# Query and key up-projections of the latent attention: columns regrouped while the weights are split, and one rotation in place of four

## What is computed

```python
(cq, ckv, kr, aq, ak, av, qi, ki, wi, rq, rk, rv, rg) = jnp.split(h @ w_in[l], split_at, axis=-1)
q = (rmsnorm(cq, g_q[l]) @ w_uq[l]).reshape(B, S, MLA_HEADS, MLA_NOPE + MLA_ROPE)    # 768 -> 8 heads x (64 + 32)
q_nope = q[..., :MLA_NOPE]
q_rope = apply_rope(q[..., MLA_NOPE:], cos_r, sin_r)
kv = (rmsnorm(ckv, g_kv[l]) @ w_ukv[l]).reshape(B, S, MLA_HEADS, MLA_NOPE + MLA_V)   # 256 -> 8 heads x (64 + 64)
k_nope, v_mla = kv[..., :MLA_NOPE], kv[..., MLA_NOPE:]
k_rope = apply_rope(kr[:, :, None, :], cos_r, sin_r)[:, :, 0]
o_a = mla_attention(q_nope, q_rope, k_nope, k_rope, v_mla)
```

## Time and profile before

| | us |
|---|---|
| median of 3 runs | 1392.13 |
| lowest and highest run | 1390.67 to 1392.34 |
| span of the profiled execution | 1389.4 |
| TensorE busy (share of the span) | 1339.9 (96%) |
| VectorE busy | 855.6 (62%) |
| ScalarE busy | 627.4 (45%) |
| GpSimd busy | 138.0 (10%) |

### The profile page before, as it was taken

How to read it: one execution, slowest core, us unless ns; L and a number is a source line. 1 busy time by engine, 2 the same in 40 slices (tenths; PEclk the granted TensorE clock), 3 DMA queues, 4 the chain that set the end, 5 groups by cost and what they waited for, 6 DMA issues and landing times.

```text
span 1389.4 us, 24758 instructions
## 1 busy us (share of the span) xinstructions
PE 1339.9 (96%) x10446; PEld 1280.1 (92%) x10446; DVE 855.6 (62%) x926; ACT 627.4 (45%) x809; POOL 138.0 (10%) x100
## 2 busy tenths in 40 slices
PE   8999999999989999999999999999999999999998
PEld 6999998789879999999888899999998878999998
DVE  5665557656557555556788765555567975655554
ACT  5443336476524443335534444444464334544442
POOL 2000003100000100002341111000025220200000
PEclk9999999999899999999999899999999989999999
DMA  8565556452225455555434134555644322455550
GB/s 261 171 210 183 183 148 176 128 152 92 90 80 171 145 183 182 181 182 171 146 89 139 61 122 155 184 184 182 178 140 139 111 93 74 169 184 181 181 181 30
DMA packets 179200, 208.83 MB, mean 150 GB/s; under 512 B 24136, under 2 KB 161984, under 8 KB 179008
## 3 DMA queue, kind: packets, MB, share of 16 engines
q1 hardware_dynamic: 178832, 207.73, 47.4%
q10 hardware_dynamic: 304, 0.20, 0.1%
HBM read 206.87 MB, written 1.05 MB: 150 GB/s over the span
## 4 chain that ended last, share of the span: by engine, by line
PE 85%; DVE 7%; ACT 3%; issue 2%; POOL 2%; DMA 1%; POOLq 0%; DVEq 0%; SPq 0%; ACTq 0%
PE bank L1661 74%; PE bank L1964 2%; PE bank L1943 2%; DVE n_lo L1326 2%; POOL scr L831 2%; PE bank L1886 1%; ACT w_hi L901 1%; DVE w_lo L1210 1%; PE bank L1950 1%; DMA raw<-in_ffn_gate_dram 1%; PE bank L1998 1%; PE bank L1937 1%; DVE hT L1347 1%; PE bank L2018 0%; PE bank L1976 0%
## 5 line engine op out<-in xcount | busy, mean ns | idle before, releaser
L1210 DVE TENSOR_TENSOR w_lo<-raw,w_hi 128x2048 fp32r<-128x2048 f32 (+1 forms) x198 | 450.9, 2279 | 297.6 <-ACT w_hi L901 296.8
L1661 PE MATMUL bank<-n_hi,w_hi 128*128 128x256 f32 x1808 | 525.0, 290 | 17.1 <-DVE n_lo L1326 8.2
L1661 PE MATMUL bank<-n_lo,w_hi 128*128 128x256 f32 x1808 | 517.9, 286 | 0.0
L1661 PE MATMUL bank<-n_hi,w_lo 128*128 128x256 f32 x1808 | 517.8, 286 | 0.0
L901 ACT ACTIVATE w_hi<-raw 128x2048 fp32r<-128x2048 f32 (+1 forms) x198 | 370.1, 1873 | 259.3 <-PE bank L1661 258.1
L1661 PEld LDWEIGHTS bank<-n_hi,w_hi 128*128 128x128 f32 x1808 | 351.9, 195 | 26.2 <-DVE n_lo L1326 11.6
L1661 PEld LDWEIGHTS bank<-n_lo,w_hi 128*128 128x128 f32 x1808 | 352.0, 195 | 0.8 <-issue 0.5
L1661 PEld LDWEIGHTS bank<-n_hi,w_lo 128*128 128x128 f32 x1808 | 352.0, 195 | 0.0
L1661 PE MATMUL bank<-hid_hi,w_hi 128*128 128x256 f32 (+1 forms) x1184 | 339.9, 287 | 2.8 <-DVE hid_lo L1618 2.1
L1661 PE MATMUL bank<-hid_lo,w_hi 128*128 128x256 f32 (+1 forms) x1184 | 336.1, 284 | 0.0
L1661 PE MATMUL bank<-hid_hi,w_lo 128*128 128x256 f32 (+1 forms) x1184 | 336.0, 284 | 0.0
(11 more groups left out here) (247 smaller groups left out, 1111.6 us busy)
## 6 DMA issues: line engine op xcount, KB each, us to landing
raw<-in_w_ff_dram SPq DMA_DIRECT2D x64, 1024.0 KB, 5.2
raw<-in_w_in_dram SPq DMA_DIRECT2D x31, 1024.0 KB, 5.4
raw<-in_ffn_gate_dram SPq DMA_DIRECT2D x22, 1024.0 KB, 5.4
raw<-in_ffn_up_dram SPq DMA_DIRECT2D x22, 1024.0 KB, 5.3
raw<-in_ffn_down_dram SPq DMA_DIRECT2D x22, 1024.0 KB, 4.9
raw<-in_w_out_dram SPq DMA_DIRECT2D x12, 1024.0 KB, 5.1
raw<-in_w_uq_dram SPq DMA_DIRECT2D x8, 576.0 KB, 4.1
raw<-in_w_in_dram SPq DMA_DIRECT2D x12, 256.0 KB, 4.0
```

Source lines behind the costliest of these rows:

```text
L1210: V.tensor_tensor(w_lo[:, s % SPLIT, 0:n], raw[:, s % RING, 0:n], w_hi[:, s % SPLIT, 0:n].bitcast(f32), ALU.subtract).then_inc(lo_ready, 1)
L1661: mm = MM(out, stat(k, a), mov(k, b), start=(first and k == 0 and n == 0), stop=(last and k == K - 1 and n == 2), skip_group_check=True)
```

## The change

The query columns are regrouped by the copies that split them, into `w_hi` and `w_lo`: first the 64 unrotated columns of all eight heads (4 blocks of 128), then the 32 rotated ones of all heads (2 blocks). The slabs are cut along the inner dimension instead of by heads: three slabs of two row blocks x 768 columns, and six output blocks, that gather over the three slabs in banks 1 to 3. Banks 1 and 2 hold the unrotated rows, which VectorE scales and writes to `qm` (new step `uqn`, four instructions on 64 rows); bank 3 holds the rotated rows of all heads, which take one rotation (`uqr`) of 128 rows, whose last sum is written as four sums of 32 rows. The `ukv` columns are regrouped in the same manner, keys first: two heads' keys share a block of 128 rows, and the values lie side by side. `proj rg` moves from before `uq` to behind the dsa scores, `uq` 0 to 2 come one after the other, and `idle[0]` is turned off at the first `uq`. Each split of a `uq` or `ukv` slab is two instructions instead of one, on ACT and on VectorE.

```diff
@@ -145,11 +145,10 @@
...
               ("topk", l, 0, 0, 8), ("idx", l, 5), ("idx", l, 6), ("proj", l, "rv"), ("rope", l, "rq"), ("idx", l, 7),
-              ("proj", l, "rg"), ("rtok", -l), ("rope", l, "kr"), ("topk", l, 1, 0, 4), ("uq", l, 0),
-              ("ret", l, 0), ("ret", l, 1), ("ret", l, 2), ("topk", l, 1, 4, 8), ("uq", l, 1), ("rope", l, "uq0"),
-              ("uq", l, 2), ("retv", l), ("rope", l, "uq1")]
-        S += attention(l, [("dsa", 0), ("dsa", 1)], [("retn", l), ("uq", l, 3)], {}, 1)
-        S += [("rety", l), ("rope", l, "uq2"), ("rope", l, "uq3")]
+              ("uq", l, 0), ("rtok", -l), ("rope", l, "kr"), ("uq", l, 1), ("topk", l, 1, 0, 4), ("uq", l, 2), ("uqn", l),
+              ("ret", l, 0), ("ret", l, 1), ("ret", l, 2), ("topk", l, 1, 4, 8), ("rope", l, "uqr"), ("retv", l)]
+        S += attention(l, [("dsa", 0), ("dsa", 1)], [("proj", l, "rg"), ("retn", l)], {}, 1)
+        S += [("rety", l)]
...
@@ -480,14 +479,16 @@
...
             elif kind == "uq":
-                _, l, n = st
+                idle[0] = False
                 slab(st)
-                job(st, of_slab=True)
-                bring(st, [(l, f"uq{n}")], (n + 1) % 2)
+                if st[2] == 2:
+                    for b in range(3):
+                        job(("uqb", st[1], b), b + 1, of_slab=(b == 2))
+                    bring(("uqb", st[1], 2), [(st[1], "uqr")], 1)
...
                 slab(st)
-                for n in range(6):
-                    job(st + (n,), of_slab=(n == 5))
+                for n in range(4):
+                    job(st + (n,), of_slab=(n == 3))
...
@@ -643,9 +644,8 @@
...
                     "kr": (src, 1, MLA_Q, "perm96", c96, krR)}
-            if name.startswith("uq"):
-                n = int(name[2])
-                return src[0:MLA_Q], 2, MLA_Q, con("perm96")[0:MLA_Q, 0:MLA_Q], [x[0:MLA_Q] for x in tab[l]["q"]], qm[0:MLA_Q, 2 * n:2 * n + 2]
+            if name == "uqr":
+                return src, 2, P, con("perm32"), tab[l]["q"], None
...
@@ -726,7 +726,18 @@
...
                 return KD * sum(n for _, n in pieces(key[1], key[2]))
-            return 6 * 192 if key[0] == "uq" else SLAB
+            return 2 * 768 if key[0] == "uq" else SLAB
+
+        def parts(s, to, of):
+
+            key = slabs[s][0]
+            if key not in ("uq", "ukv"):
+                return [(to, of)]
+            a, b = (64, 32) if key == "uq" else (64, 64)
+            to = to.rearrange("p (k c) -> p k c", k=2)
+            of = of.rearrange("p (k h c) -> p k h c", k=2, h=8)
+            return [(to[:, :, 0:8 * a].rearrange("p k (h c) -> p k h c", h=8), of[:, :, :, 0:a]),
+                    (to[:, :, 8 * a:8 * a + 8 * b].rearrange("p k (h c) -> p k h c", h=8), of[:, :, :, a:a + b])]
...
@@ -859,7 +870,7 @@
...
                     pool.wait_ge(r_ready, RN[st] + 1)
-                    scaled(st[1], "q", (con("cos_m"), con("sin_m")), rstd[:, 1, :])
+                    scaled(st[1], "q", (con("cos_i"), con("sin_i")), rstd[:, 1, :])
...
@@ -898,7 +909,9 @@
...
                 n = width(s)
-                nc.scalar.activation(w_hi[:, s % SPLIT, 0:n], raw[:, s % RING, 0:n], ACT.Copy).then_inc(hi_ready, 1)
+                for to, of in parts(s, w_hi[:, s % SPLIT, 0:n], raw[:, s % RING, 0:n]):
+                    last = nc.scalar.activation(to, of, ACT.Copy)
+                last.then_inc(hi_ready, 1)
...
@@ -1081,19 +1094,20 @@
...
                 elif kind == "uq":
-                    _, l, n = st
                     ahead(SL[st])
-                    for r in BEFORE[st]:
+                elif kind == "uqn":
+                    key = ("uqb", st[1], 2)
+                    for r in BEFORE[key]:
                         act.wait_ge(rope_done, RO[r] + 1)
-                    pb = await_bank(act, st)
-                    buf = XSC[(l, f"uq{n}")][1]
-                    nc.scalar.activation(xs[0:MLA_Q, buf, :], pb[0:MLA_Q, :], ACT.Copy, scale=MLA_Q ** -0.5).then_inc(freed(st), 1)
+                    pb = await_bank(act, key)
+                    buf = XSC[(st[1], "uqr")][1]
+                    nc.scalar.activation(xs[:, buf, :], pb[:, :], ACT.Copy, scale=MLA_Q ** -0.5).then_inc(freed(key), 1)
...
                     for t in range(NT):
-                        pb = await_bank(act, st + (4 + t,))
-                        nc.scalar.activation(vm[:, t, :], pb[:, :], ACT.Copy, scale=rtok[:, 2, t:t + 1]).then_inc(freed(st + (4 + t,)), 1)
+                        pb = await_bank(act, st + (2 + t,))
+                        nc.scalar.activation(vm[:, t, :], pb[:, :], ACT.Copy, scale=rtok[:, 2, t:t + 1]).then_inc(freed(st + (2 + t,)), 1)
...
@@ -1207,8 +1221,10 @@
...
                 n = width(s)
-                V.tensor_tensor(w_lo[:, s % SPLIT, 0:n], raw[:, s % RING, 0:n], w_hi[:, s % SPLIT, 0:n].bitcast(f32),
-                                ALU.subtract).then_inc(lo_ready, 1)
+                his = parts(s, w_hi[:, s % SPLIT, 0:n], raw[:, s % RING, 0:n])
+                for (to, of), (hi, _) in zip(parts(s, w_lo[:, s % SPLIT, 0:n], raw[:, s % RING, 0:n]), his):
+                    last = V.tensor_tensor(to, of, hi.bitcast(f32), ALU.subtract)
+                last.then_inc(lo_ready, 1)
...
@@ -1425,10 +1441,22 @@
...
                     ahead(SL[st])
-                    for n in range(4):
+                    for n in range(2):
                         pb = await_bank(dve, st + (n,))
-                        V.tensor_tensor(kfull[0:64, 2 * n:2 * n + 2, :], halves(pb[0:64, :]), rstd[0:64, 2:3, :].to_broadcast([64, 2, T]),
-                                        ALU.mult).then_inc(freed(st + (n,)), 1)
+                        for odd in range(2):
+                            r = slice(64 * odd, 64 * odd + 64)
+                            last = V.tensor_tensor(kfull[0:64, 4 * n + odd:4 * n + odd + 3:2, :], halves(pb[r, :]),
+                                                   rstd[r, 2:3, :].to_broadcast([64, 2, T]), ALU.mult)
+                        last.then_inc(freed(st + (n,)), 1)
+                elif kind == "uqn":
+                    for n in range(2):
+                        key = ("uqb", st[1], n)
+                        pb = await_bank(dve, key)
+                        for odd in range(2):
+                            r = slice(64 * odd, 64 * odd + 64)
+                            last = V.scalar_tensor_tensor(qm[0:64, 4 * n + odd:4 * n + odd + 3:2, :], halves(pb[r, :]), MLA_Q ** -0.5,
+                                                          rstd[r, 1:2, :].to_broadcast([64, 2, T]), ALU.mult, ALU.mult)
+                        last.then_inc(freed(key), 1)
...
@@ -1445,7 +1473,13 @@
...
                     dve.wait_ge(turnc_ready, r + 1)
-                    V.tensor_tensor(dst, view[2], view[0], ALU.add).then_inc(rope_done, 1)
+                    if st[2] == "uqr":
+                        for j in range(4):
+                            r32 = slice(32 * j, 32 * j + 32)
+                            last = V.tensor_tensor(qm[64:96, j:j + 5:4, :], view[2][r32], view[0][r32], ALU.add)
+                        last.then_inc(rope_done, 1)
+                    else:
+                        V.tensor_tensor(dst, view[2], view[0], ALU.add).then_inc(rope_done, 1)
...
@@ -1854,28 +1888,37 @@
...
                 elif kind == "uq":
-                    if st[2] == 0:
+                    _, l, j = st
+                    if j == 0:
                         for name in ("cq0", "cq1", "cq2", "ckv"):
-                            pe.wait_ge(*free_count(("proj", st[1], name)))
+                            pe.wait_ge(*free_count(("proj", l, name)))
+                        for b in range(3):
+                            take(pe, ("uqb", l, b))
...
                     weights(s)
-                    pb = take(pe, st)
-                    for i in range(2):
-                        mm = features(pb[0:MLA_Q, i * T:i * T + T], s, 192, i * MLA_Q, MLA_Q, K=6, xn=on)
-                    mm.then_inc(filled(st), 1)
+                    for m in range(6):
+                        out_ = bank[JOB[("uqb", l, m // 2)][0]][:, (m % 2) * T:(m % 2) * T + T]
+                        for i in range(2):
+                            k = 2 * j + i
+                            for n, (a, b) in enumerate(((0, 0), (0, 1), (1, 0))):
+                                mm = MM(out_, w(s, a)[:, i * 768 + m * P:i * 768 + m * P + P], on(k, b), start=(k == 0 and n == 0 and m % 2 == 0), stop=(k == 5 and n == 2),
+                                        skip_group_check=True)
+                        if j == 2 and m in (1, 3):
+                            mm.then_inc(filled(("uqb", l, m // 2)), 1)
+                    mm.then_inc(slab_done, 1)
...
                     weights(s)
-                    for n in range(4):
+                    for n in range(2):
...
                     for t in range(NT):
-                        pb = take(pe, st + (4 + t,))
+                        pb = take(pe, st + (2 + t,))
```

(5 more changed lines are left out.)

10 lines of the change are left out of this document (5 added, 5 removed).

## The result

The changed kernel takes 1409.85 us, median of 4 runs (1407.02 to 1413.23), against 1391.4 us of 4 runs of the kernel before beside them (1389.38 to 1392.34). The ratio is 1.0118, with a 95% interval of 1.0087 to 1.0149: slower by 12 to 21 us. The forecast was 1401, range 1386 to 1417, slower with 0.64; so the time lies in the upper half of the range, above the main course's own range (1394 to 1407).

What follows compares the result with a forecast made beforehand. TensorE was taken as the bound, VectorE having only 10 us to spare in the touched stretch; +5.5 us in layer 1 and +3.5 in layer 2 on 1392.1 gave 1401 us, range 1386 to 1417.

Steps and rivals of the forecast that it cites:

- main course: Waits and low clock in layers 1 and 2 outweigh TensorE's saving: 1401 us, own range 1394 to 1407, chance 0.50.
- Before uq 0: TensorE waits for VectorE to free rq's bank in layer 1, 3.3 us; for ACT's read in layer 2, 0.7.
- Before retv: TensorE waits for VectorE's decays: 2.5 us in layer 1, 4.7 in layer 2; the clock falls behind it.
- mla started: The first scores of mla come later than in the kernel before: +5.5 us in layer 1, +3.5 in layer 2.
- rival 2: Clock falls at the wait for key scalings, mla runs low: 10 us a layer, 1411 or 1421, chance 0.18.
- the 2.35 one: Kernel before, layer 1: TensorE's 2.35 us wait for probsT, behind which the clock was 0.50 for 10.2 us.
- low clock over retv: Clock stays down through retv and the scores: retv 5.2 us, scores 7.9 instead of 4.4.
- The rest of the kernel is the same: Outside the touched stretch of layers 1 and 2, as in the feed-forward loops, no time changes.
- Rival 3: TensorE's saving of 19.6 us comes through, VectorE making up its lag in its spare time: 1378, chance 0.10.
- Rival 1: Clock holds before retv or recovers, VectorE's chain decides: -1 us in layer 1, -3 in layer 2, 1388, chance 0.19.
- the 14 us: Estimated ceiling for all clock terms together, from the skill's under 1% of span; spoke against rival 2's full price.

Runs made afterwards that it cites:

- warm_retv: Changed kernel with 14 zero matmuls on TensorE ahead of the wait for the decays before retv: 1400.73 us, ratio to the kernel before 1.0061.
- bank_shift: Changed kernel with the count of small jobs rounded up before rotation rq, so that it has bank 0 in both layers: 1405.05 us, ratio 1.0073.
- warm_both: warm_retv with 10 more zero matmuls ahead of the wait for the key scalings before mla's first scores: 1398.03 us, ratio 1.0013.
- ret_early: Changed kernel with VectorE's decays before topk's first half, and retv waiting only for the query bank it writes to: 1398.14 us, ratio 1.0025.
- uq_only: Changed kernel with the ukv columns as before the change, so the query half alone: 1410.28 us, ratio 1.0106.
- ukv_only: Kernel before with only the ukv columns regrouped, queries and order of steps untouched: 1393.98 us, ratio 0.9997.
- before_warm: Kernel before with 10 zero matmuls ahead of its 2.35 us wait for probsT behind the dsa scores: ratio 0.9998.
- combo_a: Changed kernel with the edits of ret_early, bank_shift and pool_add, and zero matmuls ahead of four waits: 1385.7 us, ratio 0.9940.
- combo_b: combo_a with projection rg back before uq 0, and 8 zero matmuls in place of 4 before the first dsa values: 1394.95 us, ratio 1.0007.
- pool_add: Changed kernel with the four 32-row sums that end the query rotation on GpSimd instead of VectorE: 1407.87 us, ratio 1.0097.

## Why the prediction was right, and what it mis-sized

**Direction and mechanism: right.** Each wait stood where it was forecast, for the instruction that was named. Before uq 0 it was 3.68 us in layer 1 and 1.10 in layer 2 (3.3 and 0.7 forecast). Before retv it was 3.27 and 3.26 (2.5 and 4.7 forecast). The clock was 0.50 over retv and the scores. mla started at +6.8 and +4.6 us (+5.5 and +3.5 forecast). warm_retv shows that the wait before retv is a cause: with it covered, the stretch gets shorter and so does the time. For the wait before uq 0, bank_shift shows a shorter stretch (2.2 us) and no gain behind mla.

One step of layer 1 was placed too early: I let ACT copy the slab of rg right behind uq 0, but it comes behind `rtok`, so VectorE begins that split 12.0 us behind `idx` 7 and not 11.0. In layer 2 VectorE freed the bank of rq 3.4 us behind `idx` 7 and not 4.8.

**The prices that no row showed.** The strided split of a uq slab in two pieces took 1.82 us (1.75 taken), four scalings on 64 rows 2.80 (2.5), four sums on 32 rows 2.78 (2.5). The `ukv` split took 2.36 for 2048 columns in two strided pieces, 2.29 in one dense piece. So strides cost VectorE next to nothing here, and a quarter of the rows saves nothing. The Trainium skill's "VectorE: DVE Perf Modes" (Mode 1×, the baseline) says that this mode makes no assumptions, so that fp32 and odd strides work in it. It gives them no price; the rows above do.

**What was mis-sized.** The forecast was +9 us; the ratio says +16 (12 to 21), the two profiles +20.1. Of the 20.1, the two stretches account for 11.4 (9 forecast), mla for 2.4. I had priced mla at the low clock at 10 us a layer and kept it as rival 2. It came in layer 2, by the condition that I gave ("as long as the 2.35 one"), but for a quarter of that price: the clock was back after 7 us, and ACT and VectorE hid part of it. It belonged into the main sum with 2.6 us. That the time came out next to the 1411 of rival 2's one layer is chance. My reason for a low clock over retv, that small matmuls do not raise it, does not hold in general either: in layer 2 it rose within mla, 6.5 us after its start, where TensorE had only attention matmuls of 128 to 512 columns.

The other 6.3 us lie where the change does nothing: 1.5 in layer 1 ahead of `idx` 7, 3.1 there in layer 2, 1.6 in the feed-forward part between. "The rest of the kernel is the same" failed for this pair of profiles. From the matmul behind the wait of 1.56 us in layer 2 to the end of `idx` 7 it takes 25.4 us in before, warm_retv, warm_both, ret_early, uq_only and ukv_only, and 28.4 in all the others, before_warm among them, which has the kernel before's instructions there. The wait is the same in the changed kernel and in before_warm:

```profile
1077.71 1.05 PE L2047 MATMUL bank<-scr,ones 128*128 128x256 f32 x2 [1.55 <-POOL scr L842]
```

```profile
1067.14 1.16 PE L2014 MATMUL bank<-scr,ones 128*128 128x256 f32 x2 [1.56 <-POOL scr L831]
```

Here the two matmuls take 1.05 and 1.16 us and not 0.70, and the clock stays at 0.50 for 7 us. In layer 1 TensorE waits at the same place for 1.97 us in the kernel before, and the clock fell behind it in every profile: for 3.4 us in before and before_warm, for 6.8 in all the others, which cost 1.5 us more. ukv_only, which has the kernel before's instructions there, is among the others. So these are waits that the clock takes or leaves, or takes for longer, from one execution to another, and the share of it in the difference of medians stays open.

It also bears on two odd numbers at retv. Where the clock fell ahead of `idx` 7, VectorE caught up with TensorE: in layer 2 of the changed kernel it starts its first split 1.0 us behind `idx` 7, and the wait before retv is 3.3 us instead of 4.7. In warm_both, where the clock had not fallen, that split starts at 3.2 us, behind the end of topk's first part and indexer sums; this is the larger part of the 2.8 us that it was late. uq_only, where the clock had not fallen either, starts it at 3.2 us too, and waits 5.97 us before retv.

**Rivals.** Rival 3 (the saving comes through) failed by its own condition: the wait before retv was there. Rival 1 (clock held, 1388) is what warm_retv brings about by force; it came to 1400.73, since TensorE and VectorE still wait in turn elsewhere: 2.43 us before the first dsa values, behind which the clock was 0.50 for 10.3 us.

The Trainium skill's "TensorE: Matmul & The Clock Gate" (Part 1) puts the ramp's penalty under 1% of a usual kernel's span. The rows speak against it here. Covering one wait in each of two layers gained 0.6% already; and the low clock added 7.9, 7.4 and 2.6 us of TensorE time over the kernel before in the two stretches and mla, 17.9 together, over 1% of 1409.5, though a part of it lay in time that TensorE would have waited. So the 14 us that the prediction worked out from that rule was no safe bound.

## What to carry to other kernels

Before you take work from the engine that is busiest, ask whether the second engine's queue can follow; if not, the work turns into waits, and behind the longer ones (2.4 to 3.3 us here) small matmuls ran at half clock, so that a kernel with less work can be slower. Order the second engine's queue by who waits (the decays ahead of a split and four copies), keep filling between dependent steps (9 us between combo_a and combo_b), and cover what waits are left with matmuls for nobody. Judge a change of 1% from stretches of the profile beside the time: the same instructions took 25.4 or 28.4 us in a stretch that nobody had touched.

## What the hardware showed that I had not expected

mla, the same instructions in every kernel, took 18.1 to 18.4 us behind waits of up to 1.67 us, 19.4 behind waits of 1.91 to 2.48, and 20.7 to 20.9 behind 2.58 to 2.76 (the table). The granted clock goes with it: it was 1.00 over mla in the first group (but for the first 0.5 us in layer 1 of before_warm, the 18.44), 0.50 for 3.4 us at mla's beginning in the second, and for 6.8 us, from just before its start, in the third. So a tenth of a microsecond more of waiting (2.48 and 2.58) went with 1.5 us more of mla. The length of a wait is not all there is to it: ahead of retv in layer 2 of ret_early two waits of 0.75 and 0.76 us, two matmuls apart, were followed by the low clock, while before mla 1.67 us were not.

GpSimd took 5.2 us for the four sums of 32 rows in pool_add (1.3 each), VectorE 2.78:

```profile
758.30 5.20 POOL L895 TENSOR_TENSOR scr<-turn_c,turn_s 32x512 f32<-32x512 f32 x4 [8.79 <-DVE turn_s L1481]
```
